# A two-block transformer kernel in float32: a weight tile's low part on VectorE in place of GpSimd, and another order around the second block's attention

## The reference

```python
# first block, per layer                        # second block, per layer
h = rmsnorm(x, mix_norm)                        h = rmsnorm(x, norm_g)
ret, fox, rwkv, gates = split(h @ w_in)         z = h @ w_in              # 3328 columns, 13 tiles of 256
y = [retention(ret), forget_attn(fox),          o_a = attention(rope(norm(q_a)), rope(norm(k_a)), v_a)
     rwkv7_scan(rwkv)]                          o_b = windowed attention with a sink
merged = sum(sigmoid(g_i) * (y_i @ p_i))        o_c = neighbourhood attention with a bias table
x = x + merged @ w_out                          o_d = difference of two softmaxes
x = x + (silu(g) * u) @ w_down                  x = x + concat(o_i * silu(g_i)) @ w_out
```

## Time and profile before

| what | value |
|---|---|
| runs | 1157.75, 1157.89, 1158.03 us (median 1157.89) |
| the profiled execution | 1157.58 us, of which the span from the first to the last instruction is 1155.5 us |
| granted clock of TensorE, mean | 0.998 |
| busy: TensorE, VectorE, ScalarE, GpSimd | 1126.9, 767.5, 524.1, 65.7 us |
| DMA, mean | 163 GB/s |

### The profile page before, as it was taken

One profiled execution on the slowest core, in us unless ns is written; L12 is line 12 of the kernel. 1 busy time (PEld: TensorE's weight loads), 2 busy tenths in 40 slices (PEclk: granted clock), 3 DMA queues, 4 the chain that ended last, 5 costly groups with the idle time before them and its releaser, 6 DMA issues. The chain is left out here.

```text
span 1155.5 us, 21951 instructions
## 1 busy us (share of the span) xinstructions
PE 1126.9 (98%) x9400; PEld 1013.9 (88%) x9400; DVE 767.5 (66%) x1104; ACT 524.1 (45%) x734; POOL 65.7 (6%) x51
## 2 busy tenths in 40 slices
PE   5999999999999999999999999999999999999997
PEld 4789989899999998798998999999997768877785
DVE  5587765867565665787665965556667685677744
ACT  5355443534333344465334443333355565446642
POOL 1002000100000000011001000000001100030000
PEclk9999999999999999999999999999999999999999
DMA  9543335445354355443335355534436234353320
GB/s 358 222 163 110 116 109 188 176 164 224 159 218 187 144 199 187 146 146 111 111 111 220 109 219 219 216 140 189 181 141 229 109 111 182 115 218 134 116 79 37
DMA packets 27610, 188.16 MB, mean 163 GB/s; under 512 B 3472, under 2 KB 4368, under 8 KB 5776
## 3 DMA queue, kind: packets, MB, share of 16 engines
q1 hardware_dynamic: 25952, 175.89, 40.7%
q10 hardware_dynamic: 1440, 8.55, 1.9%
q0 software_dynamic: 144, 2.66, 0.6%
HBM read 181.84 MB, written 5.24 MB: 162 GB/s over the span
## 5 line engine op out<-in xcount | busy, mean ns | idle before, releaser
L669 PE MATMUL bank<-in_low,h_high 128*128 128x512 f32 x352 | 138.3, 393 | 0.0
L669 PE MATMUL bank<-in_high,h_high 128*128 128x512 f32 x288 | 117.5, 408 | 12.5 <-DVE in_low L1977 11.8
L1089 PE MATMUL bank<-h_high,gate_split 128*128 128x256 f32 x704 | 128.8, 280 | 0.2
L1089 PE MATMUL bank<-h_high,up_split 128*128 128x256 f32 x704 | 128.6, 280 | 0.0
L1105 PE MATMUL bank<-act_split,down_split 128*128 128x256 f32 x960 | 118.4, 283 | 0.0
L1105 PEld LDWEIGHTS bank<-act_split,down_split 128*128 128x128 f32 x960 | 116.6, 192 | 0.0
L694 PE MATMUL bank<-h_high,in_high 128*128 128x256 f32 x384 | 115.8, 302 | 0.5 <-DVE in_low L1851 0.5
L1378 ACT ACTIVATE in_high<-ring 128x2048 fp32r<-128x2048 f32 x47 | 89.6, 1910 | 54.9 <-PE bank L669 53.6
L669 PE MATMUL bank<-in_high,x_low 128*128 128x512 f32 x288 | 113.1, 393 | 0.0
L1089 PEld LDWEIGHTS bank<-h_high,gate_split 128*128 128x128 f32 x704 | 109.9, 189 | 0.9 <-DVE h_low L1793 0.6
L1089 PEld LDWEIGHTS bank<-h_high,up_split 128*128 128x128 f32 x704 | 109.8, 189 | 0.0
(11 more groups left out here) (348 smaller groups left out, 2385.2 us busy)
## 6 DMA issues: line engine op xcount, KB each, us to landing
ring<-w_in_dram SPq DMA_DIRECT2D x71, 1024.0 KB, 4.9
ring<-w_gate_up_dram SPq DMA_DIRECT2D x44, 1024.0 KB, 8.3
ring<-w_down_dram SPq DMA_DIRECT2D x22, 1024.0 KB, 4.8
ring<-w_out_dram SPq DMA_DIRECT2D x16, 1024.0 KB, 6.5
ring<-p_all_dram SPq DMA_DIRECT2D x6, 1024.0 KB, 4.8
x_kept<-scratch ACTq DMA_DIRECT2D x4, 1024.0 KB, 3.9
x<-x_kept ACTq DMA_DIRECT2D x4, 1024.0 KB, 8.4
table<-tables_dram POOLq DMA_DIRECT2D x1, 2594.0 KB, 11.9
```

What stands on the lines that cost most here:

```text
L669: last = mm(bank[(n - n % 2 + t) % 4][:], a, b, start=c == 0 and i == 0, stop=c == KT - 1 and i == 2)
L1089: last = mm(bank[2 * half + part][:, f * S:(f + 1) * S], a, b, start=k == 0 and i == 0, stop=k == KT - 1 and i == 2)
```

## The change

The low part of the projection's first tile moves from GpSimd to VectorE, in two halves, one ahead of `merged(1)` and one ahead of `normed(1)`. In the second block tile 5 gets a high-part buffer of its own; ScalarE no longer waits for group 2 before it makes that part, and VectorE makes the low part ahead of the wait for `b_rs` and of the rotation. In the second attention three of ScalarE's steps change places: the tanh of the gate ahead of the pair copy, the gate copy ahead of the second exponential, the high part of tile 10 behind the first two copies.

```diff
+        sb("after_lora", [P, 512])
+        in_fourth = nc.alloc_sbuf_tensor_at("in_fourth", [P, KT, 256], F32R, offset=yT_at + 4 * 512)
+        def high_of(l, n):
+            return in_fourth if n == 5 else high2[l][n % 3]
...
# TensorE, project
-  pe.wait_ge(*(wo_lo_p.after(l, 2) if q == 0 else wo_lo_v.after(l, q)))
+  pe.wait_ge(*(wo_lo_q.after(l, 2) if q == 0 else wo_lo_v.after(l, q)))
...
# ScalarE, second block
                 pair_out(l, 0)
-                next_high(l, 2)
+                in_split2(l, 5)
...
-                pair_out(l, 6)
                 act.wait_ge(*b_out.after(l, 6))
                 gate_sigmoid(l, 1280)
+                pair_out(l, 6)
                 exps, copy = attention(l, att, 4, 4, 1, lambda n: a_s[:, n % 2, :], sink=True)
                 exps(0)
+                gate_copy(1)
                 exps(1)
-                gate_copy(1)
-                next_high(l, 7)
                 copy(0)
                 copy(1)
+                next_high(l, 7)
...
# VectorE, first block
+                def first_out_low(k):
+                    dve.wait_ge(*wo_hi.after(l, k + 1))
+                    tt(wo_low[0][:, k], ring[:, SLOT1[26], k * D:(k + 1) * D], wo_high[0][:, k].bitcast(F32), ALU.subtract)\
+                        .then_inc(wo_lo_q.sem, 1)
...
                     else:
+                        first_out_low(0)
                         merged(1)
                         state_step(2, 0)
                         merged(2)
...
                         merged(3)
+                        first_out_low(1)
                         normed(1)
                         finished(1)
...
# VectorE, second block
+                in_split2(l, 5)
                 dve.wait_ge(*b_rs.after(l, 1))
...
                 rope(q_rot, q_t1, q_t2, q_rot, 6, "axial", 16).then_inc(b_rot.sem, 1)
-                for n in range(5, 7):
-                    in_split2(l, n)
+                in_split2(l, 6)
...
# GpSimd, first block
-                    if t == 1:
-                        out_low(0, 0, 1)
-                        out_low(0, 1, 2)
```

More of the change, by code:

```diff
@@ L410, in build @@
         wo_hi = sig("out_high", 5)
-        wo_lo_p = sig("out_low_pool", 2)
+        wo_lo_q = sig("out_low_first", 2)
         wo_lo_v = sig("out_low_vector", 3)
@@ L646, in split_operands @@
             def split_operands(n, l=None):
-                return (in_high[n % 2] if l is None else high2[l][n % 3]), in_low[n % 4]
+                return (in_high[n % 2] if l is None else high_of(l, n)), in_low[n % 4]
             def token_major(w, out, t):
@@ L1372, in in_split2 @@
                 act.wait_ge(*ring_in2[n % 4].after(l, n // 4 + 1))
-                f(high2[l][n % 3][:], ring[:, n % 4, :].rearrange("p (k n) -> p k n", k=KT), ACT.Copy).then_inc(in_hi2.sem, 1)
+                f(high_of(l, n)[:], ring[:, n % 4, :].rearrange("p (k n) -> p k n", k=KT), ACT.Copy).then_inc(in_hi2.sem, 1)
             def in_split(l, n, slots, done):
@@ L1826, in in_split2 @@
                 dve.wait_ge(*in_hi2.after(l, n + 1))
-                tt(in_low[n % 4][:], ring[:, n % 4, :].rearrange("p (k n) -> p k n", k=KT), high2[l][n % 3][:].bitcast(F32),
+                tt(in_low[n % 4][:], ring[:, n % 4, :].rearrange("p (k n) -> p k n", k=KT), high_of(l, n)[:].bitcast(F32),
                    ALU.subtract).then_inc(in_lo2.sem, 1)
@@ L1834, in half_split2 @@
                 last = tt(in_low[n % 4][:, k, :], ring[:, n % 4, :].rearrange("p (k n) -> p k n", k=KT)[:, k, :],
-                          high2[l][n % 3][:, k, :].bitcast(F32), ALU.subtract)
+                          high_of(l, n)[:, k, :].bitcast(F32), ALU.subtract)
                 if half:
```

## The result

The changed kernel takes 1165.74 us (median of 6 runs, 1163.40 to 1166.65); the kernel before took 1157.69 on the same chip (6 runs, 1157.42 to 1158.03). The ratio is 1.0066, 95% interval 1.0053 to 1.0079. The profiled execution took 1165.92 us with a span of 1163.8.

What follows compares the result with a forecast made beforehand. TensorE, with a matmul in flight for 98% of the span, was taken as the bound. First block +0.9, second block +3.5 and +2.7 made +7.1 us on 1157.58: 1164.7, stated as 1164.8 for the median; range 1160.8 to 1168.0.

Steps and rivals of the forecast that it cites:

- the sign: Whole kernel: slower, chance 0.84, against 0.10 for the same and 0.06 for faster.
- the likeliest case: Whole kernel: the forecast of 1164.8 us, with the collisions of VectorE and GpSimd; chance 0.70.
- First block, +0.47 a layer: First block: VectorE's second half starts 0.03 us ahead of GpSimd's power operation and delays it; TensorE 0.47 us later per layer.
- Rotation 2.1 us late by order alone: Second block: tile 5's low part, waiting for ScalarE, delays the rotation behind it on VectorE; +2.1 us per layer without collision.
- The bias collision: Second block: GpSimd's bias operations meet VectorE's last rotation operation; 4.3 us late in the first layer, 3.5 in the second.
- The clock: Second block, rival: a 5.2 us stand drops the clock, losing 1.6 us or twice that; 1166.3 to 1167.9 us, chance 0.14.
- Second attention, -0.8 a layer: Second attention: ScalarE's new order removes both L803 waits; tile 9's low part and the third weighting limit it; 0.8 us won per layer.
- That DMA is issued when group 1 is done, which the change leaves alone.: Second block: tile 5's DMA lands no sooner, so its high part still ends at 886.73; the fourth buffer gains nothing.
- the tile in time: Second block, rival: tile 5's DMA lands 2.1 us sooner, group 5 is not late; 1155.2 us, chance 0.06.

Runs made afterwards that it cites:

- The fence: Changed kernel, with VectorE made to finish the merge step before it starts the second half of the low part: 1167.47 us, ratio 1.0082.
- the bias operations late: Changed kernel, with GpSimd's two bias operations made to wait until the rotation is done: 1163.45 us, ratio 1.0045.
- tile 5 alone: Kernel before, with only the fourth high-part buffer and tile 5's low part ahead of the rotation: 1169.89 us, ratio 1.0095.

## Why the prediction was right, step by step

The time (1164.8 against 1165.74), the sign and the likeliest case held. The terms were not all right, and that the time came within 1 us is in part luck: see the third and fourth points.

- *First block, +0.47 a layer.* Right: +0.42 (the 0.3 us near 540 us was in no term). The 0.03 us by which VectorE comes first were there in both layers, and the power operation ended 0.86 us after the half. The fence shows that the order is the cause. With GpSimd first the power operation and the half took 1.01 and 1.23 us, side by side. The Trainium skill (SBUF — State Buffer, Who interferes with whom) has a VectorE instruction with two SBUF inputs and a GpSimd instruction that reads SBUF block each other, whichever comes first, for the whole instruction. The trace agrees with VectorE first (2.05 us) and not with the power operation first.
- *Rotation 2.1 us late by order alone.* Right; measured free of the collision and the low clock, 2.14 us.
- *The bias collision.* The cause and its size were right in the first layer (stand 5.12 us, I said 5.2; turn +4.4 before the clock). In the second, VectorE came first, and I had 3.5 us with 1.3 of them as a stand before the second transposes of the first attention. The low part of tile 6 was held 2.2 us, as said (4.45 us in all), but the gate's product takes its 2.86 us in the kernel before too. No such stand of over 0.4 us came in any kernel, and the turn was 2.05 us late without the clock. TensorE's scores and VectorE's first row maximum behind them, kernel before and changed kernel:

```profile
1036.63 1.13 PE L787 MATMUL bank<-scratch 64*128 64x256 f32 x8
1038.53 1.28 DVE L1919 TENSOR_REDUCE stats<-bank 128x2 f32<-128x512 f32 x2
...
1045.64 1.14 PE L793 MATMUL bank<-scratch 64*128 64x256 f32 x8
1047.60 1.27 DVE L1925 TENSOR_REDUCE stats<-bank 128x2 f32<-128x512 f32 x2
```

  The maximum follows 1.90 and 1.96 us behind the scores: it did not fall back, because the slow matmuls brought the scores later by as much. So the stand and the slow clock are not two terms to be added. Whether the 1.3 us would come at full clock stays open: where the clock stayed full (the first layer with the bias operations late), the low part of tile 6 ran free in 2.28 us.
- *The clock.* I made this a rival of 0.14 and tied it to a stand of over 4.1 us. It fell in both layers, in stands of 5.12 and 2.53 us, and cost 1.0 and 1.2 us (the turns of +5.41 and +3.25, less 4.43 and 2.05, which is how much later L1268 starts, 5.35 and 2.76, less the wait before group 5 that goes, 0.92 and 0.71). The case that happened was thus forecast and rival together; the 1.3 us that did not come and these 2.2 us partly cancel. Luck it also was that VectorE was first in the second layer, as I took it: with tile 5 alone and with the fence GpSimd was.
- *Second attention, -0.8 a layer.* Right: -0.73 and -0.80 in the changed kernel, -1.5 us in all by itself. Next in line were the low part of tile 9 (0.34 us) and the third weighing (0.41 us), as named.
- *"That DMA is issued when group 1 is done, which the change leaves alone."* The step that failed. The first half is wrong (and the ring's description says group `n - 3` where the code waits for `n - 3` finished groups, so for group `n - 4` counted from 0, which is group 1 for tile 5): the DMA is issued 0.37 us behind the vectors' DMA, and that waits for TensorE's sums. I saw the two DMAs run beside each other, looked for the reason in their sharing and gave "the tile in time" 0.06 on that account; the wait in SyncE's queue is where the lever was. The change did leave it alone, so the time came out right. The fourth buffer gained nothing, as said, but for want of the early tile I could not have told what the moved low part was worth: 2 us for the kernel, with a one-number edit to the issue order and GpSimd let go first.

What stays open: why the clock fell around stands of 2.53 and 2.65 us and not after 3.04; and which part of the spread between runs of the changed kernel (3.3 us) is the order of the two engines and which the clock. The profiled executions show both at work, but there is one of each kernel.

## What to carry to other kernels

When an operation is moved ahead of a wait, look at what its own input waits for, back to the queue that issues the DMA: a later condition of a neighbour in that queue may hold it, and no buffer helps. Where VectorE and GpSimd work within a tenth of a microsecond of each other, who starts first is a term of the sum; give the short GpSimd operation that somebody waits for a lead, by a fence if need be. A toss-up further down can hide a gain upstream, as the fence shows: judge an edit by the wait it removes, and take the toss-ups away before comparing times.

## What the runs showed of the hardware

Two GpSimd operations behave differently when GpSimd is first. Its power operation (2.27 us on 12 columns) lets VectorE's 2.29 us subtraction run beside it at full speed; its 1024-column addition, 0.11 us ahead, made a 0.96 us operation of VectorE last 3.05. Whether the operation or its size makes the difference is not shown. With VectorE first, a GpSimd operation of 12 columns went from 0.20 to 2.31 us, and the power operation from 2.27 to 4.38.

The granted clock fell in every stand of 4.8 us or more in the second block (five of them), and around two of 2.53 and 2.65 us (0.2 us before and 0.4 us after TensorE went on), but not behind 3.04, 1.65 and 1.27 us. It stayed low for 3.4 us in some and 6.8 us in others. So the length of the stand alone does not set it.
